# A hybrid decoder step on one core: a chunk's decay rows by a broadcast load instead of four matmuls

## The reference

```
xn = rmsnorm(h);  z = xn @ w_in
q, k, v = l2norm/silu(causal_conv(z...));  g = -exp(a_log) * softplus(z_a + dt_bias)
# per chunk and head:
G = cumsum(g)                                             # along the chunk's tokens
decay = exp(where(i >= j, G[i] - G[j], -inf))
lower = where(i > j, (beta * k) @ k.T * decay, 0)
u, w = solve(eye + lower, [beta * v, beta * k * exp(G)])
o = (q * exp(G)) @ S + ((q @ k.T) * decay) @ (u - w @ S);  S = ...
h = h + concat(y_a, y_b) @ w_out;  h = h + relu(rmsnorm(h) @ w_up)**2 @ w_down
```

## Time and profile before

| | before |
|---|---|
| median of 3 runs | 1426.86 us (1425.69 to 1428.42) |
| the profiled execution: time, span | 1427.06 us, 1425.3 us |
| PE busy | 1375.5 us, 97% of the span |
| DVE, ACT, POOL busy | 638.6, 323.5, 287.4 us |
| mean granted clock of PE | 0.989 of full speed |
| moved by DMA | 99.80 MB, 69 GB/s of HBM traffic over the span |

### The profile page before, as it was taken

How to read it: one execution, slowest core, us unless ns; L and a number is a source line. 1 busy time by engine, 2 the same in 40 slices (tenths; PEclk the granted TensorE clock), 3 DMA queues, 4 the chain that set the end, 5 groups by cost and what they waited for, 6 DMA issues and landing times.

```text
span 1425.3 us, 21312 instructions
## 1 busy us (share of the span) xinstructions
PE 1375.5 (97%) x8753; PEld 1341.7 (94%) x8753; DVE 638.6 (45%) x1186; ACT 323.5 (23%) x578; POOL 287.4 (20%) x214
## 2 busy tenths in 40 slices
PE   5999999899999998999999999999999999999997
PEld 4899999789999998998999999999999999999997
DVE  4367689533554535666552115531145411355123
ACT  5264541211222222222221011210012111122112
POOL 2222122211111111221222222222222222122400
PEclk9999998999999999999999999999999999999999
DMA  5123443642322222222111111121111111111312
GB/s 180 35 61 99 135 134 101 151 141 78 89 75 75 68 60 68 76 61 75 46 45 45 45 47 44 45 60 45 45 46 45 45 45 45 45 45 45 89 45 78
DMA packets 178223, 99.80 MB, mean 70 GB/s; under 512 B 19639, under 2 KB 172755, under 8 KB 178130
## 3 DMA queue, kind: packets, MB, share of 16 engines
q1 hardware_dynamic: 153600, 85.31, 21.0%
q10 hardware_dynamic: 24530, 13.13, 3.4%
HBM read 77.62 MB, written 20.80 MB: 69 GB/s over the span
## 4 chain that ended last, share of the span: by engine, by line
PE 85%; DVE 8%; issue 2%; ACT 2%; DMA 2%; POOL 1%; ACTq 0%; SPq 0%; DVEq 0%; POOLq 0%
PE bank L1094 23%; PE bank L1096 23%; PE bank L1095 23%; PE bank L1586 2%; PE bank L1588 2%; PE bank L1587 2%; DVE inverse L1862 1%; DVE outer L1860 1%; PE bank L1271 1%; PE bank L1285 1%; DVE v_feat L1657 1%; DMA decay_kept<-decay 1%; PE bank L1502 1%; DVE xn_low L1640 1%; DMA At<-At_kept 1%
## 5 line engine op out<-in xcount | busy, mean ns | idle before, releaser
L620 POOL TENSOR_TENSOR w_low<-w_raw,w_high 128x1024 fp32r<-128x1024 f32 x94 | 227.8, 2423 | 820.0 <-ACT w_high L781 820.0
L1094 PE MATMUL bank<-hg_high,w_high 128*128 128x384 f32 (+1 forms) x768 | 249.2, 325 | 1.0 <-issue 1.0
L1096 PE MATMUL bank<-hg_high,w_low 128*128 128x384 f32 (+1 forms) x768 | 247.9, 323 | 0.0
L1095 PE MATMUL bank<-hg_low,w_high 128*128 128x384 f32 (+1 forms) x768 | 247.6, 322 | 0.0
L1094 PE MATMUL bank<-xn_high,w_high 128*128 128x384 f32 (+1 forms) x672 | 229.6, 342 | 5.4 <-DVE xn_low L1640 5.4
L1095 PE MATMUL bank<-xn_low,w_high 128*128 128x384 f32 (+1 forms) x672 | 222.8, 332 | 0.0
L1096 PE MATMUL bank<-xn_high,w_low 128*128 128x384 f32 (+1 forms) x672 | 222.7, 331 | 0.0
L1094 PE MATMUL bank<-u_high,w_high 128*128 128x384 f32 (+1 forms) x576 | 186.7, 324 | 0.0
L1096 PE MATMUL bank<-u_high,w_low 128*128 128x384 f32 (+1 forms) x576 | 185.9, 323 | 0.0
L1095 PE MATMUL bank<-u_low,w_high 128*128 128x384 f32 (+1 forms) x576 | 185.7, 322 | 0.0
L781 ACT ACTIVATE w_high<-w_raw 128x1024 fp32r<-128x1024 f32 x94 | 98.7, 1049 | 257.4 <-PE bank L1096 250.6
(11 more groups left out here) (300 smaller groups left out, 1926.3 us busy)
## 6 DMA issues: line engine op xcount, KB each, us to landing
w_raw<-in_w_up SPq DMA_DIRECT2D x32, 512.0 KB, 4.1
w_raw<-in_w_down SPq DMA_DIRECT2D x32, 512.0 KB, 4.1
w_raw<-in_w_in SPq DMA_DIRECT2D x28, 512.0 KB, 4.5
w_raw<-in_w_out SPq DMA_DIRECT2D x8, 512.0 KB, 4.0
x_slice<-in_x_prompt SPq DMA_DIRECT2D x8, 512.0 KB, 4.0
out<-y_tok SPq DMA_DIRECT2D x8, 512.0 KB, 2.6
x_tok<-in_x_prompt SPq DMA_DIRECT2D x2, 1536.0 KB, 15.9
v_kept_rows<-v_feat SPq DMA_DIRECT2D x4, 536.0 KB, 3.0
```

The source lines that it names most:

```text
L620: pool.tensor_tensor(w_l[n % 2][:, :, :], w_raw[n % 2][:, :, :], w_h[n % 2][:, :, :].bitcast(F32), ALU.subtract).then_inc(w_low, 1)
L1094: pe.matmul(bank[:, 0:w], w_h[n % 2][:, k, :], hi[:, c0:c0 + w], start=(k == 0), stop=False)
L1095: pe.matmul(bank[:, 0:w], w_h[n % 2][:, k, :], lo[:, c0:c0 + w], start=False, stop=False)
L1096: ins = pe.matmul(bank[:, 0:w], w_l[n % 2][:, k, :], hi[:, c0:c0 + w], start=False, stop=(k == KT - 1))
```

## The change

The sums G are no longer made again in every partition by PE. At step G_AT = 10 one transpose on PE turns the 9 x 4 columns of -G (`gneg`) into rows, DVE negates them into `g_all` (36 x 128), and at step 11 SP writes these 18 KB to DRAM and waits for it. From there `load_g(t)` brings the four rows of a chunk into all of its partitions (128 x 512 values, 256 KB for a full chunk) into one of RB = 3 buffers in SBUF. Chunks 0 to 2 are loaded at step 11, and chunk t + 3 at step 18 + t, after DVE has read chunk t. `decay_diff` reads the buffer in place of bank 4. Four semaphores of the zero fills become one, and its waits are for all 17 fills.

```
--- before.py
+++ after.py
@@ -241,6 +241,11 @@
         At_d, X_d, Y_d = [scratch(n, [(NT - 1) * NH * P // SOLVED, BP]) for n in ("At_kept", "X_kept", "Y_kept")]
         At0_d, Y0_d = [scratch(n, [NB0, BP0]) for n in ("At0_kept", "Y0_kept")]
         D_d = scratch("decay_kept", [NT - 1, P, NH * P])
+        G_d = scratch("g_rows_kept", [NT * NH, P])
+        RB = 3
+        g_all = place("g_all", [NT * NH, P], F32, RV + SLOT)
+        g_bc = [place(f"g_broadcast{i}", [P, NH * P], F32, RV + SLOT + 512 + i * HB) for i in range(RB)]
+        assert SLOT + 512 + RB * HB <= 4 * SLOT
...
-        g_rows = sem("g_rows"); g_diff = sem("g_diff"); d_exp = sem("d_exp"); kk_made = sem("kk_made"); kk_kept = sem("kk_kept")
+        g_all_sent = sem("g_all_sent")
+        g_rows = [sem(f"g_rows{i}") for i in range(RB)]; g_diff = sem("g_diff"); d_exp = sem("d_exp"); kk_made = sem("kk_made"); kk_kept = sem("kk_kept")
...
-        pb_zero = sem("pb_zero"); x_zero = sem("x_zero"); y_zero = sem("y_zero"); y0_zero = sem("y0_zero")
+        pb_zero = sem("pb_zero"); zeroed = sem("zeroed")
...
-        ROWS_AT = 18
+        G_AT, ROWS_AT = 10, 18
         KK_AT = ROWS_AT + 1
...
+            def send_g():
+                sp.wait_ge(g_kept, 5)
+                sp.dma_start(G_d, g_all[:, :]).then_inc(g_all_sent, 16)
+                sp.wait_ge(g_all_sent, 16)
+
+            def load_g(t):
+
+                c = rows(t)
+                if t >= RB:
+                    sp.wait_ge(g_diff, t - RB + 1)
+                src = G_d[NH * t:NH * t + NH, 0:c].unsqueeze(0).to_broadcast([c, NH, c])
+                sp.dma_start(h3(heads(g_bc[t % RB], c)), src).then_inc(g_rows[t % RB], 16)
+
...
                 if g == 1 and 2 <= n < NT + 1:
-                    sp.dma_start(kept_tile(X_d, n - 1), h3(pb[6][:, :])).then_inc(x_zero, 16)
-                    sp.dma_start(kept_tile(Y_d, n - 1), h3(pb[6][:, :])).then_inc(y_zero, 16)
+                    sp.dma_start(kept_tile(X_d, n - 1), h3(pb[6][:, :])).then_inc(zeroed, 16)
+                    sp.dma_start(kept_tile(Y_d, n - 1), h3(pb[6][:, :])).then_inc(zeroed, 16)
+                if u == G_AT + 1:
+                    send_g()
+                    for t in range(RB):
+                        load_g(t)
+                if ROWS_AT <= u and u - ROWS_AT + RB < NT:
+                    load_g(u - ROWS_AT + RB)
...
                 if u == SMALL_SOLVE[-1]:
                     sp.wait_ge(solved0, 1)
-                    sp.wait_ge(y0_zero, 16)
+                    sp.wait_ge(zeroed, 16 * (2 * NT - 1))
...
-            def decay_rows(t):
-
-                c = rows(t)
-                if t:
-                    pe.wait_ge(g_diff, t)
-                else:
-                    pe.wait_ge(g_ready, 2)
-                u = upper_s if t == 0 else upper
-                for h in range(NH):
-                    ins = pe.matmul(ps[4][0:c, c * h:c * h + c],
-                                    sc["g"][0:c, t, h:h + 1].to_broadcast([c, c]), u, start=True, stop=True)
-                ins.then_inc(g_rows, 1)
+            def turn_g():
+                pe.wait_ge(g_kept, 4)
+                pe.transpose(ps[4][0:NT * NH, 0:P], sc["gneg"][:, :, :].rearrange("p t h -> p (t h)"), eye).then_inc(rows_turned, 1)
...
-                    if ROWS_AT <= u < ROWS_AT + NT:
-                        decay_rows(u - ROWS_AT)
+                    if u == G_AT:
+                        turn_g()
...
+            def keep_g():
+                dve.wait_ge(rows_turned, 3)
+                dve.tensor_scalar(g_all[:, :], ps[4][0:NT * NH, 0:P], -1.0, None, ALU.mult).then_inc(g_kept, 1)
...
-                dve.wait_ge(g_rows, t + 1)
+                dve.wait_ge(g_rows[t % RB], 16 * (t // RB + 1))
...
-                    ins = dve.scalar_tensor_tensor(out=d[0:c, c * h:c * h + c], in0=ps[4][0:c, c * h:c * h + c],
+                    ins = dve.scalar_tensor_tensor(out=d[0:c, c * h:c * h + c], in0=g_bc[t % RB][0:c, c * h:c * h + c],
                                                    scalar=sc["gneg"][0:c, t, h:h + 1], in1=ahead[0:c, :],
                                                    op0=ALU.add, op1=ALU.min)
...
+                    if u == G_AT:
+                        keep_g()
```

More of the change, by code:

```diff
@@ L505, in step @@
                     sp.wait_ge(pb_zero, 2)
-                    sp.dma_start(kept_tile0(Y0_d), h3(pb[6][0:C0, 0:NH * C0])).then_inc(y0_zero, 16)
+                    sp.dma_start(kept_tile0(Y0_d), h3(pb[6][0:C0, 0:NH * C0])).then_inc(zeroed, 16)
                 if g == 1 and 2 <= n < NT + 1:
-                    sp.dma_start(kept_tile(X_d, n - 1), h3(pb[6][:, :])).then_inc(x_zero, 16)
-                    sp.dma_start(kept_tile(Y_d, n - 1), h3(pb[6][:, :])).then_inc(y_zero, 16)
+                    sp.dma_start(kept_tile(X_d, n - 1), h3(pb[6][:, :])).then_inc(zeroed, 16)
[6 more added lines that the diff above has]
+                    load_g(u - ROWS_AT + RB)
                 if KK_AT <= u < KK_AT + NT:
@@ L541, in step @@
                     sp.wait_ge(solved, 1)
-                    sp.wait_ge(x_zero, 16 * (NT - 1))
+                    sp.wait_ge(zeroed, 16 * (2 * NT - 1))
                     sp.dma_start(kept_blocks(X_d, SOLVED, P),
@@ L545, in step @@
                     sp.wait_ge(solved_turned, 1)
-                    sp.wait_ge(y_zero, 16 * (NT - 1))
+                    sp.wait_ge(zeroed, 16 * (2 * NT - 1))
                     sp.dma_start(kept_blocks(Y_d, SOLVED, P),
@@ L1694, in ab_second @@
                                   same_s[:, 0:NS:LSEQ].unsqueeze(2).to_broadcast([C0, NSEQ, NH]), ALU.mult).then_inc(g_ready, 1)
-            nk, rk, c_, p_ = sc["nk"], sc["rk"], sc["c"], sc["p"]
             def g_keep():
@@ L1914, in keep_p @@
                     dve.wait_ge(s_levels, 16)
-                    dve.wait_ge(y_zero, 16 * (NT - 1))
+                    dve.wait_ge(zeroed, 16 * (2 * NT - 1))
                 src = ps[L_BANK][:, :].rearrange("p (h n two b) -> p h n two b", h=NH, two=2, b=b)[:, :, :, 0, :]
```

## The result

The change takes 1431.63 us (median; 1429.42 to 1435.17) where the kernel before takes 1426.50 us beside it on the same chip (1425.10 to 1428.42). The ratio is 1.0035, with a 95% interval of 1.0024 to 1.0046: 5.1 us slower, between 3.4 and 6.6. The two together give some 4.5 us, where the prediction has 2.9.

What follows compares the result with a forecast made beforehand. From 125 to 262 us the chain over DVE, ACT and SP was taken to bound, PE elsewhere. 0.2 for PE's transpose plus 2.7 on the chain gave +2.9 us, 1429.8 us; forecast's own range 1427.5 to 1432.2, overall 1424.5 to 1433.5.

Steps and rivals of the forecast that it cites:

- The stand behind POOL: DVE's decay_diff of chunks 0, 3, 6 blocks behind POOL's w_low: +1.1 us at step 18, chunks 3 and 6 nothing.
- The spill of chunk 2: SP's queue: 256 KB more delays its landing by 1.2 us; chunk 4 starts at 159.4, +2.3 us in all.
- The new wait for `decay_diff` on SP: Chunk 3's spill leaves at 161.1, after chunk 4's decay_diff, and lands at 163.9; chunk 5 starts +2.7 us late.
- What I added: Chain over DVE and SP: stand of 1.1 and spill delay of 1.2 summed, then the new wait, giving +2.7 us.
- With DVE full until 260 us: From step 24 on no load stands before a spill, and the rest moves as it is.
- PE's 9.1 us count nothing: Steps 18 to 26: PE's removed matmuls and wait, 9.1 us, gain nothing, since PE will wait for DVE instead.
- rival 1: PE's microseconds count from 125 to 180 us: 9.1 - 0.2 come off, 1418.0 us; chance 0.12.
- PE busy 7.5 us less: Profile after: PE's busy time falls some 7.5 us, with 8 to 12 us of new waits at steps 20 to 26.
- Rival 2: Idle PE falls to a lower clock; a slow piece at step 25 or 26 adds 2.5 to 5 us: 1433.5; chance 0.08.
- No gain from the place of the source: DVE's decay_diff reading SBUF instead of PSUM gets no shorter itself: no gain counted.
- rival 3: SBUF source is quicker for decay_diff on DVE: 1.7 us off, 1428.1 us; chance 0.10.
- rival 4: Loads and spills share the engines without loss and DVE's idle time swallows the rest: 1427.1 us; chance 0.12.

Runs made afterwards that it cites:

- run 1: Kernel before, with decay_diff reading k_feat in SBUF instead of bank 4, nothing loaded: 1428.24 us, ratio 1.0017.
- Run 2: The change, with decay_rows back on PE and read from bank 4, the g rows still loaded but unread: 1429.45 us, ratio 1.0020.
- run 4: Kernel before, with a memset and six scratch products added on DVE just ahead of the full solve: 1430.49 us, ratio 1.0030.
- run 3: Kernel before, without PE's decay_rows of chunks 2 to 8, which read chunk 1's rows: 1425.15 us, ratio 0.9995.
- run 9: The change, with PE's decay_rows made as well into bank 4, where nobody reads them: 1429.90 us, ratio 1.0030.
- run 5: The change, with the g-row loads moved behind both spills and the gather in SP's step: 1431.63 us, ratio 1.0034.
- run 10: The change, with loads behind the spills and gather, and PE's unread decay_rows made as well: 1427.74 us, ratio 1.0009.
- run 6: The change, with six g-row buffers instead of three, so no loads in steps 21 to 23: 1428.28 us, ratio 1.0005.
- run 7: The change, with decay_diff of chunks 0, 3 and 6 ahead of squares_low on DVE: 1431.71 us, ratio 1.0024.
- run 8: The change, with six buffers and decay_diff of chunks 0, 3 and 6 ahead of squares_low: 1426.25 us, ratio 0.9988.
- the change again: The unaltered change timed once more against the kernel before, on the chip of the next three kernels: 1430.14 us, ratio 1.0027.

## Why the prediction was right and where it was off

The direction was right: slower was the likeliest sign, by the chain over DVE and SP, and the time lies in the range. The size was off: +2.9 was forecast, +5.1 and +3.9 were measured. The interval of the second (2.3 to 5.6) holds 2.9, that of the first (3.4 to 6.6) doesn't. That the forecast of the chain comes out so close (+2.7 forecast, +2.8 in the profile) is in part luck: two sizes in it were off against each other, as the third point says. Point by point:

- *The stand behind POOL, +1.1 us at step 18.* Right. Chunks 0, 3 and 6 took 2.92, 3.28 and 3.25 us, and alone (run 1) they put the solve back by 1.0 to 1.2 us. That those of chunks 3 and 6 are covered was right as well.
- *The spill of chunk 2, +1.2 us for 256 KB.* Mis-sized. It left at 154.32 (154.4 forecast), but landed after 4.14 us, not 5.0, and chunk 4 started at 158.66 instead of 159.4.
- *The new wait for `decay_diff` on SP.* The mechanism was right, the two sizes in it were off against each other. The spill of chunk 3 left at 160.21, not 161.1, and took 4.3 us, not 2.8. I had taken the 2.1 us of a lone spill for one that has a load ahead and, behind it, another spill and a gather. My own rows spoke against it: this same spill took 4.93 us before, and a later one 5.18. The landing was at 164.5; issued at 161.1 and with 4.93 it would have been at 166.0, and the forecast had 163.9. Both bounds of the range kept the 2.1. Chunk 5 started at 164.54 (163.95 forecast).
- *What I added.* The stand and the late spill were summed to +2.7 for the chain, and it was +2.8 in the profile. Run 2 shows that the loads bring 2.9 alone. So the stand at step 18 adds nothing to the loads: it only takes the place of waiting for the spill of chunk 2 that would be there.
- *"With DVE full until 260 us" the rest moves as it is.* Right up to the end of the projection: its last products start 2.6 and 2.1 us late in the two profiles of the change, with the solve late by 2.8 and 2.4. What lies behind takes 1.6 and 0.6 us longer, at a granted clock of 0.91 instead of 0.96 from 540 to 580 us. Between 1 and 2 us of what was measured isn't accounted for by the chain, and the forecast had no term for it: it moved the part after 262 us as it was. In run 4, a pure delay, that part was 1.6 us longer too. Since the clock was the same in both profiles of the change and the loss wasn't, and a profile is one execution, the cause of this part stays open.
- *PE's 9.1 us count nothing* (rival 1 falls). Right: run 3 took 6.2 us away for -0.7, and run 9 gave 7.6 us back at no cost in time. The waits for the kept products were 8.4 us, within the 8 to 12 forecast.
- *PE busy 7.5 us less.* Right between 120 and 180 us, wrong over the span: 1375.7 against 1375.5 us in one profile of the change, 1371.3 in the other. Part or all of what went there came back at the lower clock. Rival 2 had seen the clock but not that it would eat so much of PE's saving; whether it costs time on top is what runs 5, 9 and 10 leave open.
- *No gain from the place of the source* (rival 3 falls). The groups that don't stand take 1.14 us from SBUF, and took 1.13 from PSUM. The Trainium skill's table of fixed costs (VectorE: DVE Perf Modes, "The TRN2 errata") would have them shorter, by an estimate from it some 0.26 us for four operations (62 cycles each); the traces don't agree.
- *Nothing reaches the chain* (rival 4 falls).

## What to carry to other kernels

A transfer that waits for a consumer, put into an in-order queue ahead of one that others wait for, hands its wait on; six buffers instead of three, so that no such load falls into the tight steps, was worth more here than any other edit. Moving one input of a DVE operation from PSUM to SBUF, where the other lies in SBUF already, made it stand behind a GpSimd operation of 2.5 us, so look at what POOL does in that moment, and whether the operation can go into DVE's own wait just ahead. Two delays that end in the same wait are not to be summed, and work taken from an engine that is busy for 97% of the span was worth nothing that could be measured where another engine leads (run 3).

## What I had not expected

The stand has a mirror. POOL's copy of 24 columns at about 142 us, which took 0.49 us before, took 2.01 in the change, just over the time in which DVE did a tap (141.56), its short piece (142.76) and `decay_diff` of chunk 2 (142.93), all of them now with two tensors of SBUF; the rows are in the two timelines above. It ended at 144.12, with DVE's last such operation at 144.06; the gaps between DVE's operations didn't let it in. The Trainium skill's rule (SBUF — State Buffer, "Who interferes with whom"), that the second to come blocks until the first is over, holds in this direction too, and over a row of short operations, not only one. Runs 5 to 8 and the change again show the same 2.01 us, runs 9 and 10 1.47. Run 1 is an exception: with the same three operations on DVE its copy began at 142.63 and took 0.31, so there it got in between them. Nothing on the chain waited for it.

And a PE with 7.2 us less to do in 60 us was no less busy over the whole span in one profile, and only 4.2 us less in another, because its lower clock took back all or part of what the work had been.
